# First modulation by channel tile on four column groups of TensorE, with four convolution tiles accumulating together

## What is computed

```python
sh1, sc1, g1, sh2, sc2, g2 = jnp.split((s_lat @ ada_w[i] + ada_b[i])[:, None, :], 6, axis=-1)
hx = x * (1 + sc1) + sh1
...
    csh1, csc1, cg1, csh2, csc2, cg2 = jnp.split(s_ctx @ ada_w[i] + ada_b[i], 6, axis=-1)
    hc = ctx * (1 + csc1) + csh1
...
        xbc = jax.nn.silu(depthwise_conv_grid(proj[..., :SSM_CONV_DIM], conv_w, conv_b, rows_, cols_))
        dt = jax.nn.softplus(proj[..., SSM_CONV_DIM:].astype(f32).reshape(bb, LL, 2, SSM_HEADS)
                             + dt_bias.astype(f32))
```

## Time and profile before

| | us |
|---|---|
| three timed runs | 1849.37, 1851.29, 1851.89 |
| median | 1851.29 |
| span of the profiled execution | 1848.9 |
| median less that span | 2.4 |

### The profile page before, as it was taken

How to read it: one execution, slowest core, us unless ns; L and a number is a source line. 1 busy time by engine, 2 the same in 40 slices (tenths; PEclk the granted TensorE clock), 3 DMA queues, 4 the chain that set the end, 5 groups by cost and what they waited for, 6 DMA issues and landing times.

```text
span 1848.9 us, 18264 instructions
## 1 busy us (share of the span) xinstructions
PE 1651.8 (89%) x5432; PEld 907.8 (49%) x5432; DVE 1447.5 (78%) x3491; ACT 595.6 (32%) x1483; POOL 538.8 (29%) x543
## 2 busy tenths in 40 slices
PE   8999999999989987989899999999999878777776
PEld 3787688544544433334333778546444433322332
DVE  6788995877677778988887789887777788777755
ACT  4565754232222223333322221122223233222222
POOL 0343000034333333333343000133334333333332
PEclk9999999999999999999999999989999999999998
DMA  9333249899999999999999666699999999999996
GB/s 363 138 123 134 114 169 364 335 371 427 427 424 427 427 426 426 394 425 427 422 422 425 238 265 225 253 427 426 427 426 427 427 427 423 425 423 420 424 427 254
DMA packets 96423, 664.34 MB, mean 359 GB/s; under 512 B 11421, under 2 KB 13438, under 8 KB 17476
## 3 DMA queue, kind: packets, MB, share of 16 engines
q0 software_dynamic: 74304, 536.90, 69.4%
q1 hardware_dynamic: 22020, 126.27, 17.7%
HBM read 662.02 MB, written 1.11 MB: 359 GB/s over the span
## 4 chain that ended last, share of the span: by engine, by line
PE 46%; DMA 30%; DVE 16%; issue 3%; ACT 3%; PEld 1%; POOL 0%; PEldq 0%; DVEq 0%; POOLq 0%; SPq 0%; ACTq 0%
DMA expert_rows<-in_p_uv,chosen_experts 25%; PE bank L1202 16%; DVE dot_products L2597 6%; PE bank L943 4%; DMA expert_rows_spare<-in_p_uv,chosen_experts 4%; PE bank L1336 4%; PE bank L1158 3%; PE bank L983 3%; PE bank L1060 3%; PE bank L1418 1%; PE bank L998 1%; PE bank L875 1%; ACT weight_diagonal L1763 1%; DVE conv_work_or_state L2131 1%; PE bank L1368 1%
## 5 line engine op out<-in xcount | busy, mean ns | idle before, releaser
L1202 PE MATMUL bank<-expert_rows,weight_diagonal 128*128 128x512 f32 x1816 | 852.8, 611 | 146.1 <-ACT weight_diagonal L1763 145.6
L2597 DVE SCALAR_TENSOR_TENSOR dot_products<-expert_rows,bank 128x1024 f32<-128x1024 f32 x454 | 554.2, 1221 | 210.5 <-DMA expert_rows<-in_p_uv,chosen_experts 198.4
L1202 PEld LDWEIGHTS bank<-expert_rows,weight_diagonal 128*128 128x128 f32 x1816 | 337.2, 193 | 598.9 <-issue 346.6
L1469 POOL DMA_INDIRECT expert_rows<-in_p_uv,chosen_experts x450 | 423.3, 941 | 697.4 <-PE bank L1202 653.7
L1763 ACT ACTIVATE weight_diagonal<-constants,expert_weights 128x128 f32<-128x128 f32 x512 | 178.0, 394 | 240.7 <-DVE expert_weights L2525 239.6
L1755 ACT ACTIVATE expert_gelu<-expert_dots 128x2 f32<-128x2 f32 x260 | 52.8, 203 | 608.4 <-DVE dot_products L2597 608.1
L1469 POOL DMA_INDIRECT expert_rows_spare<-in_p_uv,chosen_experts x58 | 54.5, 939 | 463.1 <-DVE chosen_experts L2510 369.9
L1202 PE MATMUL bank<-expert_rows_spare,weight_diagonal 128*128 128x512 f32 x232 | 112.4, 608 | 21.8 <-ACT weight_diagonal L1763 21.8
L2597 DVE SCALAR_TENSOR_TENSOR dot_products<-expert_rows_spare,bank 128x1024 f32<-128x1024 f32 x58 | 70.8, 1221 | 25.0 <-DMA expert_rows_spare<-in_p_uv,chosen_experts 23.3
L1478 POOL TENSOR_TENSOR weights_lo<-weight_block,weights_hi 128x1024 fp32r<-128x1024 f32 x22 | 53.1, 2416 | 119.4 <-ACT weights_hi L1525 119.4
L1202 PEld LDWEIGHTS bank<-expert_rows_spare,weight_diagonal 128*128 128x128 f32 x232 | 42.8, 193 | 75.8 <-issue 41.5
(11 more groups left out here) (345 smaller groups left out, 2067.9 us busy)
## 6 DMA issues: line engine op xcount, KB each, us to landing
weight_block<-in_ada_rows SPq DMA_DIRECT2D x25, 1024.0 KB, 6.2
weight_block<-in_m_in_blocks SPq DMA_DIRECT2D x20, 1024.0 KB, 6.8
hyena_weight_block<-in_h_in_blocks SPq DMA_DIRECT2D x12, 1024.0 KB, 6.6
hyena_weight_block<-in_ada_rows SPq DMA_DIRECT2D x12, 1024.0 KB, 6.8
weight_block<-in_wq_blocks SPq DMA_DIRECT2D x11, 1024.0 KB, 6.9
expert_rows<-in_p_uv,chosen_experts POOLq DMA_INDIRECT x450, 14.0
out_weights<-in_m_out_blocks SPq DMA_DIRECT2D x6, 1024.0 KB, 7.7
weight_block<-in_ada_shift SPq DMA_DIRECT2D x4, 1024.0 KB, 10.6
```

Of the source, the lines that this page charges most:

```text
L1202: last = mm(ps[b][:, :], dg[n % DIAG][:, :], uv[slot][:, D + h * 512:D + (h + 1) * 512], start=(r == 0 and k == 0), stop=end)
L1469: pool.indirect_dma_start(uv[slot][:, :], None, A[f"p_uv{l}"], bass.IndirectOffsetOnAxis(ap=chosen[:, s_, k:k + 1], axis=0)).then_inc(uv_l ...
L2597: stt(prod[:, :], uv[slot][:, 0:D], 1.0, rows_t, ALU.mult, ALU.mult, accum_out=dots[:, s_, k + j:k + j + 1]).then_inc(sem("dots_done"), 1)
```

## The change

The modulation is made per channel tile `k`. A new layout of the weights, `ada_front`, holds for each `k` all 1024 rows of its 128 shift and 128 scale columns (1 MB). The SiLU columns are padded to 32 columns for each of the eight row tiles `j`, and product `j` writes to 32 PSUM partitions, those of group `j % 4`. ACT copies the 128 x 256 sums, TensorE adds the four groups with `group_sum` (this also turns rows into columns), DVE adds the bias, and the tile is modulated and split at once. The products of four convolution tiles with tile `k` follow as soon as it is split, in four banks. There are four buffers of hi and lo weights (`SPLITS = 4`), so ACT makes `weights_hi` of tile q+4 in its round for tile q. `step_rows` uses both halves of the step weights as one stationary operand of 128 columns, 16 products for 24. Transposes, decays and running sums stand one tile later on TensorE. `CONV_DOTS`, and the ring's order after its first blocks, stay as they were.

```diff
...
-FRONT_ROWS = 3
+FRONT_TILES = 4
+COL = 32
 Z_DOTS = (2,) * 8
 CONV_TILES = (16, 17, 18, 19, 0, 1, 2, 3, 4, 5, 6, 7, 20, 21, 8, 9, 10, 11, 12, 13, 14, 15, 22, 23)
 CONV_WITH_CTX = tuple(q for q, ct in enumerate(CONV_TILES) if ct < CTX_CT)
 OUT_BLOCKS = INNER // P // 2
 CONV_DOTS = tuple((1, m, q) for m, q in enumerate((1, 1, 2, 3, 4, 5, 6, 7, 13, 14, 15, 16, 17, 18)))
 FRONT_DOTS = len(CONV_DOTS) + KD
-HELD_GATE_ROWS = (FRONT_ROWS, FRONT_ROWS + 1)
+HELD_GATE_ROWS = (0, 1)
+SPLITS = 4
 DEFERRED = 2
 SCAN_DOTS = KD - 4
 BIG = 1.0e30
 MASKED = 2.0 ** 100
 TINY = 2.0 ** -120
+TRANSPOSED_AFTER = {4: (), 5: (0,), 6: (1,), 7: (2,), 8: (3,), 9: (4,), 10: (5, 6)}
...
-        front(0)
-        sp.dma_start(cst[:, C_ID, :], A["constants"][:, 0:P]).then_inc(sem("identity_in"), 16)
...
+            sp.dma_start(hT[:, k, :], A["tokens_T"][:, k * 2 * T:(k + 1) * 2 * T]).then_inc(sem(f"tokens{k}_in"), 16)
+            if k < FRONT_TILES // 2:
+                weights(at("xbc", k), at("xbc", k) + 1)
         sp.dma_start(wdt, A["dt_weights"].rearrange("p (k c) -> p k c", k=KD)).then_inc(sem("dt_weights_in"), 16)
         sp.dma_start(dtb[:], A["m_dt_bias"].rearrange("o a b -> (a b) o")).then_inc(sem("dt_in"), 16)
-        weights(6, 7)
+        weights(4, 7)
         sp.dma_start(cst[:, 1:7, :], A["constants"][:, P:7 * P].rearrange("p (a b) -> p a b", a=6)).then_inc(sem("constants_in"), 16)
         sp.dma_start(aneg[:], A["m_a_log"].rearrange("o a b -> (o a b)").partition_broadcast(P)).then_inc(sem("scan_rows_in"), 16)
         sp.dma_start(dskip[:], A["m_d"].rearrange("o b -> (o b)").partition_broadcast(P)).then_inc(sem("scan_rows_in"), 16)
-        weights(7, at("ada0_rows", FRONT_ROWS + 2))
+        weights(7, at("ada0_rows", 2))
...
+        def front_products(k):
+
+            if k < 2:
+                block_in(pe, place["front", k])
+            else:
+                pe.wait_ge(sem(f"front_rows{k}_in"), 16)
+            b = begin(("front_sums", k))
+            for j in range(KD):
+                g = slice(COL * (j % 4), COL * (j % 4 + 1))
+                last = mm(ps[b][g, 0:2 * P], s_col[:, j, :], front_rows[k][:, j * 2 * P:(j + 1) * 2 * P], start=(j < 4), stop=(j >= 4))
+            last.then_inc(full[b], 1)
+
+        def front_columns(k):
+
+            wait_read(pe, ("front_sums", k))
+            b = begin(("front_columns", k))
+            for n in range(2):
+                last = mm(ps[b][:, 2 * n:2 * n + 2], front_sums[k % 2][:, n * P:(n + 1) * P], group_sum, start=True, stop=True)
+            last.then_inc(full[b], 1)
+
+        def input_products(q, k):
+
+            c0 = 0 if q in CONV_WITH_CTX else T
+            b = begin(("xbc", q)) if k == 0 else plan(("xbc", q))[0]
+            for n, (lhs, rhs) in enumerate(((whi, hThi), (whi, hTlo), (wlo, hThi))):
+                last = mm(ps[b][:, c0:2 * T], lhs[q % SPLITS][:, k, :], rhs[:, k, c0:2 * T], start=(k + n == 0), stop=(k == KD - 1 and n == 2))
+            if k == KD - 1:
                 last.then_inc(full[b], 1)
...
+        pe.wait_ge(sem("group_sum_set"), 1)
+        for k in range(KD):
+            front_products(k)
+            if k >= 1:
+                front_tiles((0, 1), k - 1)
+            front_columns(k)
+            if 2 <= k <= 4:
+                front_tiles((2, 3), k - 2)
+            if k >= 4:
+                front_tiles((2, 3), k - 1)
+        front_tiles((0, 1), KD - 1)
+        front_tiles((2, 3), KD - 1)
...
-                for n, (lhs, rhs) in enumerate(((dthi, hThi), (dthi, hTlo), (dtlo, hThi))):
-                    last = mm(ps[b][0:2 * HEADS, :], lhs[:, k, :], rhs[:, k, :], start=(k + n == 0), stop=(k == KD - 1 and n == 2))
+                for n, rhs in enumerate((hThi, hTlo)):
+                    last = mm(ps[b][:, :], dtw_split[:, k, :], rhs[:, k, :], start=(k + n == 0), stop=(k == KD - 1 and n == 1))
             last.then_inc(full[b], 1)
...
-        for q in range(XBC_CT):
+        step_rows()
+        for q in range(FRONT_TILES, XBC_CT):
             pe.wait_ge(*lo_made(q))
...
-            if q == 1:
-                step_rows()
-            elif q == 3:
+                input_products(q, k)
+            if q == FRONT_TILES:
                 step_columns()
-            elif q == 12:
+            elif q == 13:
                 decay_sums()
-            elif q == 14:
+            elif q == 15:
                 running_sums()
-            conv_transposes(q - 3)
-        conv_transposes(XBC_CT - 3)
+            for r in TRANSPOSED_AFTER.get(q, (q - 4,)):
+                conv_transposes(r)
+        for r in range(XBC_CT - 4, XBC_CT - 2):
+            conv_transposes(r)
 
...
+        pool.memset(s_col, 0.0).then_inc(sem("silu_c_cleared"), 1)
         for q in range(LO_BY_VECTOR, XBC_CT):
             pool.wait_ge(sem("weights_hi"), q + 1)
-            wait_full(pool, ("xbc", q - 2))
-            pool.tensor_tensor(wlo[q % 2][:, :, :], half_block("xbc", q), whi[q % 2][:, :, :].bitcast(F32), ALU.subtract).then_inc(sem("weights_lo"), 1)
+            wait_full(pool, ("xbc", q - SPLITS))
+            pool.tensor_tensor(wlo[q % SPLITS], half_block("xbc", q), whi[q % SPLITS].bitcast(F32), ALU.subtract).then_inc(sem("weights_lo"), 1)
         peer(0)
...
-            if k >= 2:
-                act.wait_ge(sem("context_modulated"), k - 1)
-                act.wait_ge(sem("latent_modulated"), k - 1)
-                f(hThi[:, k - 2, :], hT[:, k - 2, :], ACT.Copy).then_inc(sem("mixer_input_hi"), 1)
-        weights_hi("xbc", whi, 1, xbc_used)
+        def weights_hi(q):
+
+            block_in(act, place["xbc", q // 2])
+            if q >= SPLITS:
+                wait_full(act, ("xbc", q - SPLITS))
+            f(whi[q % SPLITS], half_block("xbc", q), ACT.Copy).then_inc(sem("weights_hi"), 1)
...
+
+        def front_split(k):
+
+            act.wait_ge(sem("latent_modulated"), k + 1)
+            act.wait_ge(sem("context_modulated"), k + 1)
+            f(hThi[:, k, :], hT[:, k, :], ACT.Copy).then_inc(sem("mixer_input_hi"), 1)
+
+        for k in range(KD):
+            copy_out(("front_sums", k), front_sums[k % 2], lambda b: b[:, 0:2 * P])
+            act.wait_ge(sem(f"tokens{k}_in"), 16)
+            wait_read(act, ("front_columns", k))
+            f(hT[:, k, 0:T], hT[:, k, 0:T], ACT.Identity, scale=front_mod[:, k, 1, 1:2], bias=front_mod[:, k, 0, 1:2]).then_inc(sem("context_modulated"), 1)
+            front_split(k)
+            for q in range(2 * k, min(2 * k + 2, FRONT_TILES)):
+                weights_hi(q)
...
-            if q == 2:
+            if q == 1:
                 act.wait_ge(sem("dt_in"), 16)
-                copy_out("dt_rows", dtrow, lambda b: b[0:2 * HEADS, :], ACT.Identity, bias=dtb[:, 0:1])
+                b = wait_full(act, "dt_rows")
+                f(dtrow[0:2 * HEADS, :], ps[b][0:2 * HEADS, :], ACT.Identity, bias=dtb[:, 0:1])
+                f(dtrow[2 * HEADS:P, :], ps[b][2 * HEADS:P, :], ACT.Copy).then_inc(read[b], 1)
             elif q == 5:
...
-                if q + 2 < XBC_CT:
-                    weights_hi("xbc", whi, q + 2, xbc_used)
+                if q + SPLITS < XBC_CT:
+                    weights_hi(q + SPLITS)
             r = q - 3
...
-                tt(hTlo[:, k - 3, :], hT[:, k - 3, :], hThi[:, k - 3, :].bitcast(F32), ALU.subtract).then_inc(sem("mixer_input_lo"), 1)
-        weights_lo(1)
+        for k in range(KD):
+            b = wait_full(dve, ("front_columns", k))
+            tt(front_mod[:, k, :, :], ps[b][:, 0:4].rearrange("p (n j) -> p n j", n=2), front_bias[:, :, k:k + 1].to_broadcast([P, 2, 2]), ALU.add).then_inc(read[b], 1)
+            wait_read(dve, ("front_columns", k))
+            dve.wait_ge(sem(f"tokens{k}_in"), 16)
+            ts(hT[:, k, T:2 * T], hT[:, k, T:2 * T], front_mod[:, k, 1, 0:1], front_mod[:, k, 0, 0:1], ALU.mult, ALU.add).then_inc(sem("latent_modulated"), 1)
+            dve.wait_ge(sem("mixer_input_hi"), k + 1)
+            tt(hTlo[:, k, :], hT[:, k, :], hThi[:, k, :].bitcast(F32), ALU.subtract).then_inc(sem("mixer_input_lo"), 1)
+            for q in range(2 * k, min(2 * k + 2, FRONT_TILES)):
+                weights_lo(q)
         dve.wait_ge(sem("dt_weights_hi"), 1)
         tt(dtlo, wdt, dthi.bitcast(F32), ALU.subtract).then_inc(sem("dt_weights_lo"), 1)
...
```

236 lines of the change are left out of this document (77 added, 159 removed).

## The result

| | us |
|---|---|
| before, median (4 runs beside those of the changed kernel) | 1851.59 |
| changed, median (4 runs, 1886.30 to 1890.10) | 1887.22 |
| ratio, 95% interval | 1.0199, 1.0185 to 1.0214 |
| span of the profiled execution, before and after | 1848.9, 1884.5 |

The changed kernel is slower by 2.0%. The forecast was 1877 with 1860 to 1889, so the range held the time; it lies 10 us above the middle, outside the 1871 to 1883 of the middle case alone. The spans differ by 35.6 us, and all of it is there when the scan's first products are through: the products of line 1022, which follow them, start at 236.60 us, and the same ones (line 1010) at 200.96 before.

What follows compares the result with a forecast made beforehand. TensorE paces the 24-tile convolution pipeline, DVE close behind. Terms 15.5 - 20.8 + 11.2 + 9.2 + 4.1 + 7.3 = 26.5 us; span 1848.9 + 26.5 = 1875.4, plus 2.4, about 1877 us, range 1860 to 1889.

Steps and rivals of the forecast that it cites:

- middle case: Modulation products of the front partly side by side on TensorE: 1.95 us a set, about 1877 us; chance 0.42.
- DVE's tile 1: DVE starts tile 1 at 63.5 us instead of 48.02, behind the front, step_rows and ACT's copies: +15.5 us.
- waits after tile 1 gone: With TensorE running ahead, DVE's waits after tile 1 go: -20.8 us, all that there is.
- (1): ACT asks for block x9 behind centre tap 14, so centre tap 15 waits behind tile 18's split: +11.2 us.
- (2): ACT asks for block x10 behind centre tap 16 and waits for its landing, at tile 20's split: +9.2 us.
- (3): SiLU of tile 14 is late, so tile 17's transposes reach DVE's weigh_first of tile 20 late: +4.1 us.
- (4): Tile 13 waits for the decays, 4.5 us, and tile 9 for transposes, 2.8 us: together +7.3 us.
- the prediction's signs: Two DVE waits for centre taps, about 11 and 9 us, with ACT waiting for a block 2.6 us less.
- The front: Modulation and the first four convolution tiles: TensorE bounds rounds of 5.15 us, and four tiles are done at 57.6 us.
- four abreast: Rival: four column groups run side by side, a set costs 0.9 us, the chain's 4.15 is the round: 1871; chance 0.15.
- Nothing else is on the chain: Beyond the listed terms no cost: DVE's front dots go but ran beside TensorE's modulation products; ada_rows blocks stay as many.
- Moves as a whole: The scan's chain behind the taps, engines waiting for engines, only shifts with them: no added time.

Runs made afterwards that it cites:

- ACT's order alone: The changed kernel with ACT making weights_hi two tiles ahead, not four, from tile 18 on, so centre taps 15 to 17 come first: 1876.59 us.
- the ring's dots alone: The changed kernel with the dots m = 8 to 11 at tiles 10 to 13 and not 13 to 16: 1872.71 us, ratio 1.0118.
- the last experiments: The changed kernel with four edits together, 1854.04 us; then that kernel with ACT's step-size copies ahead of centre tap 3, not 2, 1851.38 us.
- the four edits: The changed kernel with the scan's banks turned, early dots, late step sizes, and transposes of tiles 5, 16, 17 one tile earlier: 1854.04 us, ratio 1.0013.

## Why the prediction was right, and what it left out

| step | forecast | measured |
|---|---|---|
| DVE's tile 1 | +15.5 | 58.53 - 48.02 = +10.5 |
| waits after tile 1 gone | -20.8 | -(24.5 - 3.34) = -21.2 |
| (1) split of tile 18 | +11.2 | +10.06 |
| (2) split of tile 20 | +9.2 | +7.29 |
| (3) transposes of tile 17 | +4.1 | +5.13 |
| (4) tiles 9 and 13 | +7.3 | 5.28 + 4.68 = +10.0 |
| dots and `weigh_first` beside GpSimd | none | (26.9 - 18.9) + (4.9 - 4.5) = +8.4 |
| the scan's first products | none | +5.7 |

The measured rows add up to 35.9 for 35.6. All old waits are counted as gone, with a sixth of 0.4 us that the earlier trace rows leaves out, and the new ones in full: at tile 13 and ahead of tile 20 there had been waits of 3.3 and 3.7 before. The 5.7 is what the step to 236.60 leaves over: 35.6, less 10.5, less 19.5 between tile 1 and the end of the second `x_weighted` (158.9 us for 139.4). Two small slips don't matter: 9 x 0.22 is 1.98 and not 1.95, and 1875.4 + 2.4 is 1877.8.

**The held centre taps** were right in place and cause, shown twice: by ACT's order alone and by the ring's dots alone. Both prices were a little high: from the end of the dot at 148.68 to the split of tile 18 at 155.97 passed 7.3 us and not 8.6, and x10 landed in 4.76 us and not in 6.8. ACT stood longer than the prediction's signs said (13.06 and 12.68 us for about 8.6 and 6.4), because it arrived at the splits earlier; that costs nothing, since the blocks' arrival ends the wait.

**The front** took the middle case, and that step failed: four groups do run side by side, with a set of 1.07 us where the middle case wanted 1.95. The rival of four abreast named the time 1.0 us a round less; it was 5.15 - 4.43 = 0.7 in five rounds, and the first ones went faster as well, though the first two sets did take 1.94 and 1.93 us. The Trainium skill, TensorEngine Tiling (Array Packing), Theoretical Speedup, gives up to four times for 32 columns; this case has 3.64 / 1.07 = 3.4. The rule of the Trainium skill, TensorE: Matmul & The Clock Gate, Part 3, on program order, to which I gave weight, doesn't keep the groups apart. So the case that held was the rival of 1871 with a chance of 0.15, and its time misses the measured one by 16 us.

**"Nothing else is on the chain"** is the sentence that failed most. It counted DVE's dots as many as before, each 1.22 us, and didn't ask what GpSimd would be doing beside them. Before, GpSimd made one `weights_lo` about every 6 us in step with the tiles, and 2 of the 14 dots took longer than 1.3 us; in the changed kernel `weights_lo` comes in bunches (three in 8.10 us from 59.52 on), and 7 do. The experiment with the short `weights_lo` shows the cause and prices all of it at 13.7 us, of which 8.4 came with the change; that the four buffers make the bunches is argued, not shown, since the kernels of the last experiments have four as well and their dots take 20.1 and 20.2. The dots scatter from 26.9 to 28.9 us among the kernels that leave their surroundings as they are.

**"Moves as a whole"** failed too: the scan's chain hung on banks, and the diff moved them. This stood in the planner's table of banks, which I had read for the convolution and not for what comes after it.

**The waits for transposes** (4) were larger at tile 9, and in the four edits they go when tile 5's transposes stand one tile earlier.

**TensorE's clock** isn't in the prediction behind the front, and it has a part in these waits. Columns as in the earlier trace rows, the changed kernel and then the kernel before:

```profile
95.00:140.00 45.00, 33.55 (x176) 28.74 (x177) 34.58 (x87) 24.52 (x34) 12.47 (x6) 0.81 0.29 110
80.00:125.00 45.00, 45.00 (x253) 38.83 (x252) 37.44 (x92) 29.75 (x43) 17.83 (x9) 1.00 0.40 141
```

In the changed kernel TensorE stands still from 95 to 100 us, waiting for DVE's taps to free a bank; the granted clock is 0.61 there and 0.50 in the 5 us after it, and the 24 products that start at 103.82 take 8.53 us and not 5.50. DVE's wait at tile 9 ends behind them. In the kernel with late step sizes they take 5.81 and that wait is 2.1 us for 5.28. Ahead of tile 20 the chain of the changed kernel and that of the kernel with turned banks say:

```profile
176.50 7.90 PE bank L874 x24
...
176.70 6.42 PE bank L874 x24
```

From 176 to 184 us the granted clock was 0.66 in the first and 0.85 in the second. The tile is 1.5 us shorter there and DVE's last dot before the wait 1.25 longer (2.47 for 1.22), which makes the wait for `x_tokens` 2.4 us for 5.13, and makes the second `x_weighted` start 1.24 us earlier. No run changes the clock alone, so its share in the whole is not measured.

In sum the span came out 1884.5 - 1875.4 = 9.1 us above the forecast: 8.4 and 5.7 were missing, the front was 5.0 too dear, 0.4 more was given back, and the waits of (1) to (4) came out 0.6 above their 31.8; that makes 9.3, and 0.2 is not accounted for. So the place and cause of the larger part, the held taps, were foreseen, but that the range held the time is partly luck: 14.1 us that were put at nothing lay against 5.0 us too much.

What stays open: the wait for `x_tokens` ahead of tile 20 was 2.4 to 6.8 us in the experiments, a race between TensorE's last tiles and DVE that is followed above for two kernels only; the same front gave DVE's tile 1 at 58.5 to 60.6 us in five kernels, so the +10.5 carries a scatter of about 2 us; and no kernel kept the whole of `weights_lo` away from the dots, so what a better order of the two would bring is not measured.

## What to carry to other kernels

More buffers let a producer run ahead, but an engine that asks for a late block in program order holds everything behind the request: check what stands behind each request, and what releases the block. When a change regroups banks or buffers, follow each one to its next user in the next stage. When the time of GpSimd's work moves, DVE's instructions with only SBUF operands may change their length though their number doesn't (here 18.9 to 26.9 us for 14 dots), so compare mean durations by line before looking for waits.

## What the runs showed of the hardware

- Eight products of 32 stationary columns and 256 moving ones (16 records, 32-bit floats) took 1.07 us in four column groups (the first two sets of the kernel 1.94 and 1.93) and 3.64 us in one.
- DVE's dot of 128 x 1024 from two SBUF operands took 1.22 us alone and up to 3.3 beside a GpSimd subtraction of the same size (2.4 us alone); a tap of 128x189 that reads PSUM stayed at about 405 ns.
- A tensor-by-scalar operation of 128 x 256 in SBUF took 0.29 us alone and 2.42 us beside GpSimd.
- In the changed kernel 5 us with TensorE busy for 1.50 were followed by 8 us granted 0.50; in the kernel with turned banks 5 us with 1.49 were followed by 8 us granted 1.00. The 24 products of a tile took 5.50 us at a granted clock of 1.00 and 7.90 where 8 us were granted 0.66 on average.
